# Stick-breaking attention layer: the first projections in rounds of 256 tokens, and q of the first half before k and v of the second

## The chip, the cores and the metric

The kernel runs on one core of a Trainium2 chip. The metric is the device time of one execution in microseconds. Before the change it is 693.96 us, the median of three runs (693.77 to 694.22).

## What is computed

One layer of a trunk with 1024 tokens and width 1024, all in float32:

```python
h = x * rsqrt(mean(x * x, -1) + eps) * norm_g
q, k, v, gate = split(h @ w_in, 4)              # 16 heads of 64
z = q @ k.T / 8
log_beta = log_sigmoid(z)
log_1m = where(key < query, log_beta - z, 0)
after = reverse exclusive cumsum of log_1m over keys
a = where(key < query, exp(log_beta + after), 0)
o = (a @ v) * silu(gate)
x = x + o @ w_out
out = x * rsqrt(mean(x * x, -1) + eps) * final_g
```

## The kernel before

The 16 heads are taken as 8 pairs. The engines run programs of their own, joined by semaphores; in each program a pair is 16 slots, and in the slots of one pair k, v, q and the gate of the next pair are projected in between. TensorE (PE) multiplies in a rounded float32 format; to keep precision each operand is split into a high and a low half, and a product is three matmuls (high by high, high by low, low by high).

Before the slots lies a prologue. It makes hT, the scaled and transposed input, of the eight x blocks of 128 tokens, and projects k, v and q of the first pair, 512 tokens ("a half") at a time.

- **Loads.** SP loads the odd x blocks and the w pieces (L374 to L382, two pieces of 4 x 128 rows for each of k, v, q), ACT the even x blocks (L672). Raw w always lies in w_raw, which has room for two pieces, so that a piece waits for the split of the one two before it (L361).
- **Scaling.** ACT squares blocks 0, 2, 4, 6, 7 (L684) and DVE 1, 3, 5 (L886), each with a sum along the row. A root is taken for blocks 0 to 3 and one for 4 to 7: ACT's square root (L676) and six small DVE instructions (rsqrt, L866). Blocks 3, 6 and 7 are scaled on ACT (L703), the others on DVE (L892).
- **hT.** PE transposes four blocks at a time, 128 columns each, into one of four PSUM banks (transpose_x, L511: 16 units, 8 of each half). ACT writes the high half with the gain (hi_x, L691), DVE the low half (lo_x, L897). A bank is free for unit n when unit n-4's low half is done.
- **Weights.** DVE casts the high half of each piece (next_w, L905), POOL subtracts it from the raw one for the low half (lo_w, L1109).
- **Projections.** In the order of PROLOGUE (L145): k, v of half 0, k, v of half 1, q of both. Each is 8 blocks of 3 matmuls of 512 columns (project, L494), in turns in proj_ps and o_ps. Units 4 to 7 are transposed between the blocks of the first, 8 to 15 between those of the second. ACT copies each result to stage (to_stage, L727), in program order with all its other work; projection h waits until result h-2 is there (L531). DVE splits k and q out of stage (heads_hi, heads_lo, L932, L942), and PE transposes v from there (transpose_v, L502), behind the third and the fifth projection.
- **PE's warm-up.** WARM_UP transposes of the identity (L524) run behind ACT's first square, ahead of the x transposes.
- **Slot 0** (L611): its own part of a projection first, then the scores (L578), which wait for all of q and k and for the copy of k with its heads swapped (swap_k, L366).

The planner at the top (plan, L38) and the order of slots are not touched.

## Time and profile before

| what | us |
|---|---|
| median of 3 runs | 693.96 (693.77 to 694.22) |
| the profiled execution, its own time | 693.87 |
| its span, first to last instruction | 692.1 |
| PE, DVE, ACT, POOL busy | 670.1, 480.0, 426.2, 280.2 |
| mean granted TensorE clock | 0.997 |

The profile is one execution. Times in its rows count from the start of the span. PE is a matmul, PEld its weight load; matmuls are pipelined, so that a row's duration is longer than its share of a stream. An idle time in brackets stands before the instruction, with what ended it.

### The profile page before, as it was taken

How to read it: one execution, taken by the hardware profiler on the slowest of the kernel's cores; microseconds unless marked ns; L12 is line 12 of the kernel's file. 1: busy time of each engine (PE TensorE's matmuls, PEld its weight loads, DVE VectorE, ACT ScalarE, POOL GpSimd, SP SyncE). 2: the span in 40 equal slices, each digit the busy share in tenths (PEclk: the TensorE clock that was granted, in tenths of full speed). 3: DMA queues.
4: the chain of work that ended last, by engine and by line, in shares of the span. 5: the costliest groups of instructions: out<-in, count | busy, mean ns of one | idle time of the engine just before them, and what ended most of it. 6: DMA issues, size and time to landing. Idle time of an engine off the chain costs nothing.

```text
span 692.1 us, 10879 instructions
## 1 busy us (share of the span) xinstructions
PE 670.1 (97%) x3426; PEld 563.5 (81%) x3426; DVE 480.0 (69%) x637; ACT 426.2 (62%) x795; POOL 280.2 (40%) x225
## 2 busy tenths in 40 slices
PE   5999999999999999999999999999999999999995
PEld 5787888888888888888888888888888777887784
DVE  5835666786778667766776677777776799644765
ACT  5614667676767676766676667666767685532432
POOL 2122435454454445544545363626353643324200
PEclk9999999999999999999999999999999999999998
DMA  7131311141115100420042014111421179222432
GB/s 289 46 90 48 92 31 31 55 129 33 31 30 139 46 19 30 121 76 15 30 122 63 28 32 121 61 31 30 121 62 30 61 239 320 96 92 65 162 124 91
DMA packets 28123, 57.65 MB, mean 83 GB/s; under 512 B 3376, under 2 KB 3376, under 8 KB 28080
## 3 DMA queue, kind: packets, MB, share of 16 engines
q1 hardware_dynamic: 25312, 51.13, 24.3%
q10 hardware_dynamic: 2736, 6.03, 2.3%
q8 instruction: 16, 0.26, 0.2%
q14 instruction: 27, 0.22, 0.1%
q0 software_dynamic: 32, 0.00, 0.0%
HBM read 37.23 MB, written 11.53 MB: 70 GB/s over the span
## 4 chain that ended last, share of the span: by engine, by line
PE 89%; DVE 6%; ACT 1%; issue 1%; DMA 1%; POOL 0%; POOLq 0%; ACTq 0%; DVEq 0%
PE proj_ps L497 46%; PE o_ps L643 10%; PE z_ps L592 9%; PE t_ps L655 9%; PE z_ps L572 6%; PE proj_ps L572 4%; PE o_ps L497 2%; DVE rest L1035 2%; PE t_ps L506 1%; PE z_ps L525 1%; DVE hT L901 1%; DMA a_group<-x 1%; DVE gate L1017 1%; PE z_ps L517 1%; DVE arena L981 1%
## 5 line engine op out<-in xcount | busy, mean ns | idle before, releaser
L497 PE MATMUL proj_ps<-hT,w_split 128*128 128x512 f32 x1464 | 359.9, 394 | 2.1 <-DVE hT L901 1.4
L497 PEld LDWEIGHTS proj_ps<-hT,w_split 128*128 128x128 f32 x1464 | 269.9, 188 | 57.6 <-DVE hT L901 2.3
L1136 POOL TENSOR_TENSOR a_group<-a_group,rest 128x128 f32<-128x128 f32 (+7 forms) x128 | 158.0, 1234 | 302.1 <-DVE rest L1035 302.1
L1035 DVE TENSOR_TENSOR_SCAN rest<-rest,restart 128x128 f32<-128x128 f32 (+7 forms) x128 | 204.4, 1597 | 16.4 <-ACT rest L820 16.0
L805 ACT ACTIVATE aT<-t_ps 128x512 fp32r<-128x512 f32 (+2 forms) x160 | 80.0, 531 | 62.8 <-PE t_ps L655 61.4
L1001 DVE TENSOR_TENSOR aT<-t_ps,aT 128x512 fp32r<-128x512 f32 (+2 forms) x160 | 93.0, 606 | 36.9 <-ACT aT L805 35.4
L1112 POOL TENSOR_TENSOR w_split<-w_raw,w_split 128x512 fp32r<-128x512 f32 x64 | 91.6, 1432 | 37.9 <-DVE w_split L863 37.9
L592 PE MATMUL z_ps<-arena 128*128 128x512 f32 (+2 forms) x384 | 96.4, 366 | 0.3 <-DVE arena L950 0.3
L950 DVE TENSOR_TENSOR arena<-stage,arena 64x512 fp32r<-64x512 f32 x64 | 43.9, 686 | 67.9 <-ACT arena L750 67.3
L820 ACT ACTIVATE rest<-z_ps 128x128 f32<-128x128 f32 (+7 forms) x128 | 83.8, 655 | 9.6 <-PE z_ps L592 9.3
L643 PE MATMUL o_ps<-aT,arena 128*128 128x512 f32 (+2 forms) x320 | 82.6, 364 | 2.8 <-DVE aT L1001 2.8
L822 ACT ACTIVATE a_group<-z_ps 128x128 f32<-128x128 f32 (+7 forms) x128 | 84.3, 659 | 0.0
L655 PE MATMUL t_ps<-ident,a_group 128*128 128x128 f32 x576 | 83.7, 272 | 0.5 <-POOL a_group L1136 0.5
L655 PEld LDWEIGHTS t_ps<-ident,a_group 128*128 128x128 f32 x576 | 69.2, 141 | 8.8 <-issue 0.9
L730 ACT ACTIVATE stage<-proj_ps 128x512 f32<-128x512 f32 x61 | 36.5, 599 | 61.0 <-PE proj_ps L497 61.0
L643 PEld LDWEIGHTS o_ps<-aT,arena 128*128 128x128 f32 x320 | 59.7, 188 | 17.5 <-DVE aT L1001 4.8
L592 PEld LDWEIGHTS z_ps<-arena 128*128 128x128 f32 x384 | 59.6, 190 | 5.2 <-DVE arena L950 0.8
L572 PE MATMUL z_ps<-arena,hT 128*128 128x512 f32 x246 | 58.4, 392 | 0.9 <-DVE a_group L1081 0.6
L797 ACT ACTIVATE oT<-o_ps 64x512 f32<-64x512 f32 x32 | 19.0, 593 | 59.5 <-PE o_ps L643 59.5
L572 PEld LDWEIGHTS z_ps<-arena,hT 128*128 128x128 f32 x246 | 45.5, 188 | 11.0 <-POOL arena L314 1.9
L991 DVE TENSOR_TENSOR oT<-o_ps,oT 64x512 f32<-64x512 f32 x32 | 22.0, 688 | 25.2 <-ACT oT L797 24.9
L757 ACT ACTIVATE w_split<-w_raw 128x512 fp32r<-128x512 f32 x56 | 35.9, 641 | 0.5
(89 smaller groups left out, 458.1 us busy)
## 6 DMA issues: line engine op xcount, KB each, us to landing
w_raw<-w_in SPq DMA_DIRECT2D x64, 256.0 KB, 2.6
arena<-arena SPq DMA_DIRECT2D x32, 256.0 KB, 4.3
wo_raw<-w_out SPq DMA_DIRECT2D x16, 256.0 KB, 3.9
o_hi_scratch<-o_split SPq DMA_DIRECT2D x14, 256.0 KB, 2.1
o_lo_scratch<-o_split SPq DMA_DIRECT2D x14, 256.0 KB, 2.4
hT<-o_hi_scratch SPq DMA_DIRECT2D x14, 256.0 KB, 5.8
hT<-o_lo_scratch SPq DMA_DIRECT2D x14, 256.0 KB, 6.5
a_group<-x SPq DMA_DIRECT2D x13, 256.0 KB, 3.3
```

Source lines behind the costliest of these rows:

```text
L497: mm = nc.tensor.matmul(bank[:, :], w_split[:, ring, wl, b, :], hT[:, hl, b, half * HALF:(half + 1) * HALF], start=(b == 0 and n == 0), st ...
L572: mm = nc.tensor.matmul(bank[:, :], hT[:, ol, b, tokens], w_out_of(nh, wl)[:, b, :], start=(b == first and m == 0), stop=(b == last and m ...
L592: mm = nc.tensor.matmul(z[:, c0:c1], q, k_of(par, hh, swapped)[:, c0 - first:c1 - first], start=not swapped, stop=swapped)
L643: mm = nc.tensor.matmul(o_ps[:, c:HALF], v_of(apar)[:, j, 2 * ahh:2 * ahh + 2, :] .rearrange("p x d -> p (x d)"), moving, start=(j == 0 an ...
L655: last = nc.tensor.transpose(t_ps[t % 2][:, i2 * P:(i2 + 1) * P], a_g[grp][:, i2, j * P:(j + 1) * P], ident[:, :])
L805: nc.scalar.activation(to, t_ps[t % 2][:, rel * P:HALF], ACT.Copy).then_inc(t_hi, 1)
L820: nc.scalar.activation(rest[:, s % 2, S - width:S], z_ps[s % 2][:, first:first + width], ACT.Sigmoid, scale=-SCALE).then_inc(rest_ready, 1)
L822: nc.scalar.activation(a_g[grp][:, i % GQ, 0:width], z_ps[s % 2][:, first:first + width], ACT.Sigmoid, scale=SCALE).then_inc(beta_ready, 1)
L1001: nc.vector.tensor_tensor(lo, t_ps[t % 2][:, rel * P:HALF], hi.bitcast(F32), ALU.subtract).then_inc(t_lo, 1)
L1035: nc.vector.tensor_tensor_scan(span, span, restart[:, S - 1:(S - 1 - width if width < S else None):-1], 0.0, ALU.mult, ALU.max).then_inc(s ...
L1112: nc.gpsimd.tensor_tensor(to[:, 1], w_raw[:, part, :].rearrange("p (b n) -> p b n", b=4), to[:, 0].bitcast(F32), ALU.subtract).then_inc(w_ ...
L1136: nc.gpsimd.tensor_tensor(a, a, rest[:, s % 2, S + 1 - width:S + 1], ALU.mult).then_inc(a_ready, 1)
```

## The change

- **Two rounds of 256 tokens.** The first half's units are now 16, of two blocks and 256 columns each (X_UNITS); the second half's stay 8 of four blocks. PE projects k, then v of tokens 0 to 255, then k, then v of tokens 256 to 511, with 256-wide matmuls, then q of half 0, and after that k, v, q of half 1. Units 4 to 15 stand between the blocks of the rounds, units 16 to 23 between those of q.
- **Three roots.** Blocks 0 and 1, 2 and 3, 4 to 7 have a root each. Block 1 is squared on DVE and scaled on ACT, block 2 squared and scaled on DVE, block 3 squared and scaled on ACT. The small instructions of the second root stand one by one between low halves of units 4 to 7.
- **Weights.** v's raw pieces are loaded into stage, q's are split into a quarter of the arena that is free until then. ACT casts k's first piece; SP and ACT load w pieces between the x blocks.
- **PE.** The warm-up has 54 transposes and doesn't wait for a square; 4 more (STILL_WARM) follow the first four units. The transpose of v's second half moves behind slot 0's own projection.
- **k swap.** It waits for three splits instead of two, since q's now stands between those of k.
- **Memory.** The buffer rest is allocated behind ident; what lay between shifts by its size.

The diff, cut to its core (a "..." is left-out lines):

```diff
-PROLOGUE = (("k", 0), ("v", 0), ("k", 1), ("v", 1), ("q", 0), ("q", 1))
-
-X_ACT, X_DVE = (3, 6, 7), (0, 1, 2, 4, 5)
+PROLOGUE = (("k", 0), ("v", 0), ("q", 0), ("k", 1), ("v", 1), ("q", 1))
+ROOTS = 3
+
+X_ACT, X_DVE = (1, 3, 6, 7), (0, 2, 4, 5)
 X_SCALED = [(1, X_ACT.index(b) + 1) if b in X_ACT else (0, X_DVE.index(b) + 1) for b in range(KB)]
-WARM_UP = 34
+WARM_UP = 54
+STILL_WARM = 4
+
+
+X_UNITS = [(b, 0, 2) for b in range(KB)] + [(b, 2, 2) for b in range(KB)] + [(b, GQ, GQ) for b in range(KB)]
+UNITS_X = len(X_UNITS)
...
-        rest = sb("rest", [P, 2, S + 1])
...
         ident = sb("ident", [P, P])
+        rest = sb("rest", [P, 2, S + 1])
...
+        wq_split = arena[:, 1, 3, :].rearrange("p (l b n) -> p l b n", l=2, b=KB)
+
+        def first_raw(n):
+
+            home = stage[:, n % 2, :] if n in (2, 3) else w_raw[:, n % 2, :]
+            return home.rearrange("p (b n) -> p b n", b=4)
+
+        def first_w(n):
+
+            unit, part = n // 2, n % 2
+            to = wq_split if unit == 2 else w_split[:, unit % 2]
+            return to[:, 0, 4 * part:4 * part + 4, :], to[:, 1, 4 * part:4 * part + 4, :]
+
+        def x_unit(u):
+
+            b, first, count = X_UNITS[u]
+            return b, slice(first * P, (first + count) * P), z_banks[u % 4][:, 0:count * P]
...
+        def load_first_w(eng, n):
+
+            eng.dma_start(first_raw(n).rearrange("p b n -> p (b n)"), w_in[(KB, 2 * KB, 0)[n // 2], n % 2, :, :]
+                          ).then_inc((wv_loaded if n in (2, 3) else w_loaded)[n % 2], 16)
+
+        def wait_first_w(eng, n):
+
+            if n in (2, 3):
+                eng.wait_ge(wv_loaded[n % 2], 16)
+            else:
+                eng.wait_ge(w_loaded[n % 2], 16 * max(n // 2, 1))
...
-                sp.wait_ge(qk_split, 4 * p + 2)
+                sp.wait_ge(qk_split, 4 * p + (3 if is_first(p) else 2))
...
-            for b in (1, 3):
+            load_x_block(sp, 1)
+            load_first_w(sp, 0)
+            load_x_block(sp, 3)
+            for n in (2, 3):
+                load_first_w(sp, n)
+            for b in (5, 7):
                 load_x_block(sp, b)
-
-            kinds = (1, 2, 0)
-            for n in range(2 * UNITS0):
-                load_w(n, n % 2, n % 2, kinds[n // 2] * KB)
-                if n == 1:
-                    for b in (5, 7):
-                        load_x_block(sp, b)
+            for n in (4, 5):
+                sp.wait_ge(w_ready, n - 3)
+                load_first_w(sp, n)
...
+            def transpose_x(u):
+                b, first, count = X_UNITS[u]
+                wait(pe, xt_lo, u - 3)
+                for i in range(count):
+                    scaled, done = X_SCALED[first + i]
+                    pe.wait_ge((x_scaled, x_scaled_act)[scaled], done)
+                    last = nc.tensor.transpose(z_banks[u % 4][:, i * P:(i + 1) * P],
+                                               x_blocks[first + i][:, b * P:(b + 1) * P], ident[:, :])
...
+            def project_first(unit, bank, cols, b):
+
+                weights = wq_split if unit == 2 else w_split[:, unit]
+                for n, (wl, hl) in enumerate(((0, 0), (0, 1), (1, 0))):
+                    mm = nc.tensor.matmul(bank, weights[:, wl, b, :], hT[:, hl, b, cols],
+                                          start=(b == 0 and n == 0), stop=(b == KB - 1 and n == 2))
+                return mm
...
-            pe.wait_ge(x_squared, 1)
             for n in range(WARM_UP):
                 nc.tensor.transpose(z_banks[0][:, 0:P], ident[:, :], ident[:, :])
-            for n in range(4):
-                transpose_x(n)
+            for u in range(4):
+                transpose_x(u)
+            for n in range(STILL_WARM):
+                nc.tensor.transpose(t_ps[0][:, 0:P], ident[:, :], ident[:, :])
+
+            for quarter in range(2):
+                for unit, bank in enumerate((proj_ps, o_ps)):
+                    cols = slice(quarter * 2 * P, (quarter + 1) * 2 * P)
+                    for b in range(KB):
+                        pe.wait_ge(xt_lo, KB * quarter + b + 1)
+                        pe.wait_ge(w_ready, 2 * unit + b // 4 + 1)
+                        mm = project_first(unit, bank[:, cols], cols, b)
+                        if quarter == 0 and b // 4 == unit:
+                            transpose_x((4, 8)[unit] + b % 4)
+                        if quarter == 1 and unit == 0 and b < 4:
+                            transpose_x(12 + b)
+                    if quarter == 1:
+                        mm.then_inc(proj_done, 1)
...
+                if h < 2:
+                    continue
                 wait(pe, stage_ready, h - 1)
                 for b in range(KB):
-                    pe.wait_ge(xt_lo, KB * half + b + 1)
-                    pe.wait_ge(w_ready, 2 * unit + b // 4 + 1)
-                    mm = project(unit % 2, (proj_ps, o_ps)[h % 2], half, b)
-                    if h == 0 and b < 4:
-                        transpose_x(b + 4)
-                    if h == 1:
-                        transpose_x(KB + b)
+                    pe.wait_ge(xt_lo, 2 * KB + (b + 1 if half else 0))
+                    pe.wait_ge(w_ready, 2 * "kvq".index(kind) + b // 4 + 1)
+                    mm = project_first("kvq".index(kind), (proj_ps, o_ps)[h % 2][:, :],
+                                       slice(half * HALF, (half + 1) * HALF), b)
+                    if h == 2:
+                        transpose_x(2 * KB + b)
                 mm.then_inc(proj_done, 1)
-                if h in (2, 4):
-                    transpose_v(h // 2 - 1, h // 2 - 1, h - 1, 1)
+                if h == 2:
+                    transpose_v(0, 0, 1, 1)
...
+                        pe.wait_ge(xt_lo, UNITS_X)
...
                     project_part(p, s)
+                    transpose_v(1, 1, 4, 0)
...
-            for b in range(0, KB, 2):
+            for b in (0, 2):
+                load_x_block(act, b)
+            load_first_w(act, 1)
+            for b in (4, 6):
                 load_x_block(act, b)
...
+            def hi_x(u):
+                b, cols, bank = x_unit(u)
+                act.wait_ge(xt_done, u + 1)
+                nc.scalar.activation(hT[:, 0, b, cols], bank, ACT.Copy, scale=g_col[:, b:b + 1]).then_inc(xt_hi, 1)
+
+            def scale_x(b, number):
+
+                act.wait_ge(rstd_ready, 5 * number)
+                nc.scalar.activation(x_blocks[b], x_blocks[b], ACT.Copy, scale=rstd[:, b:b + 1]
+                                     ).then_inc(x_scaled_act, 1)
+
+            def hi_first_w(n):
+
+                wait_first_w(act, n)
+                nc.scalar.activation(first_w(n)[0], first_raw(n), ACT.Copy).then_inc(w_hi, 1)
...
             square_x(0, 0)
-            square_x(1, 2)
+            act.wait_ge(x_squared_dve, 1)
+            root(slice(0, 2), x_squared, 1)
+            hi_first_w(0)
+            scale_x(1, 1)
+            act.wait_ge(g_loaded, 16)
+            for u in range(4):
+                hi_x(u)
+            square_x(1, 3)
+            hi_x(4)
             act.wait_ge(x_squared_dve, 2)
-            root(slice(0, 4), x_squared, 2)
+            root(slice(2, 4), x_squared, 2)
+            for u in range(5, KB):
+                hi_x(u)
             square_x(2, 4)
-
-            def scale_x(blocks):
-                for b in blocks:
-                    nc.scalar.activation(x_blocks[b], x_blocks[b], ACT.Copy, scale=rstd[:, b:b + 1]
-                                         ).then_inc(x_scaled_act, 1)
-
-            act.wait_ge(rstd_ready, 5)
-            scale_x(X_ACT[:1])
-            act.wait_ge(g_loaded, 16)
-            for n in range(KB):
-                hi_x(n)
-                if n in (3, 4):
-                    square_x(n, n + 3)
-                if n == 5:
-                    act.wait_ge(x_squared_dve, 3)
-                    root(slice(4, 8), x_squared, 5)
-            act.wait_ge(rstd_ready, 10)
-            scale_x(X_ACT[1:])
+            scale_x(3, 2)
+            for u in range(KB, 2 * KB):
+                hi_x(u)
+                if u == KB + 3:
+                    square_x(3, 6)
+            act.wait_ge(x_squared_dve, 4)
+            root(slice(4, 8), x_squared, 4)
+            scale_x(6, 3)
+            scale_x(7, 3)
...
+                if h in (2, 4, 5):
+                    act.wait_ge(qk_split, {2: 1, 4: 2, 5: 3}[h])
+                if h < 2:
+                    act.wait_ge(w_ready, 3 + h)
+                if h == 3:
+                    act.wait_ge(t_done, 1)
                 to_stage((proj_ps, o_ps)[h % 2], h, h % 2)
-                if h == 0:
-                    for n in range(KB, 2 * KB):
-                        hi_x(n)
-                if h in (3, 5):
-                    v_hi(0, h // 2 - 1, h // 2 - 1, h // 2 - 1)
+                if h == 1:
+                    for u in range(2 * KB, UNITS_X):
+                        hi_x(u)
+                    v_hi(0, 0, 0, 0)
...
+            v_hi(0, 1, 1, 1)
...
-                        act.wait_ge(qk_split, 3 + half)
+                        act.wait_ge(qk_split, 4)
+                        act.wait_ge(t_done, 2)
...
+            def next_w(n):
+                wait_first_w(dve, n)
+                nc.vector.tensor_copy(first_w(n)[0], first_raw(n)).then_inc(w_hi, 1)
...
             square_x(0, 1)
-            square_x(1, 3)
             dve.wait_ge(table_loaded, 1)
+            dve.wait_ge(x_squared_dve, 1)
+            dve.wait_ge(x_squared, 1)
+            rsqrt(slice(0, 2), 0)
+            scale_x(X_DVE[:1])
+            square_x(1, 2)
+            dve.wait_ge(g_loaded, 16)
+            for u in range(4):
+                lo_x(u)
+                if u in (1, 3):
+                    next_w((u + 1) // 2)
+            dve.wait_ge(x_squared, 2)
             dve.wait_ge(x_squared_dve, 2)
-            dve.wait_ge(x_squared, 2)
-            rsqrt(slice(0, 4), 0)
-            scale_x(X_DVE[:3])
-            next_w(0)
-            next_w(1)
-            dve.wait_ge(g_loaded, 16)
-            for n in range(KB):
-                lo_x(n)
-                if n == 2:
-                    square_x(2, 5)
-                    next_w(2)
-                if n == 3:
+            root_of_second = rsqrt_steps(slice(2, 4), 1)
+            for u in range(4, KB):
+                next(root_of_second)
+                lo_x(u)
+                if u == KB - 3:
                     next_w(3)
-                if n == 6:
-                    dve.wait_ge(x_squared, 5)
-                    dve.wait_ge(x_squared_dve, 3)
-                    rsqrt(slice(4, 8), 1)
-            scale_x(X_DVE[3:])
+            for _ in root_of_second:
+                pass
+            scale_x(X_DVE[1:2])
+            square_x(2, 5)
+            for u in range(KB, 2 * KB):
+                lo_x(u)
+                if u == KB + 3:
+                    square_x(3, 7)
+                if u in (KB + 5, KB + 6):
+                    next_w(u - KB - 1)
+            dve.wait_ge(x_squared, 4)
+            dve.wait_ge(x_squared_dve, 4)
+            rsqrt(slice(4, 8), 2)
+            scale_x(X_DVE[2:])
...
             for h, (kind, half) in enumerate(PROLOGUE):
-                if h in (2, 4, 5):
+                if h == 1:
+                    for u in range(2 * KB, UNITS_X):
+                        lo_x(u)
+                        if u == 2 * KB + 2:
+                            heads_hi("k", 0, 0, 0, 0)
+                            heads_lo("k", 0, 0, 0, 1)
+                    v_lo(0, 0, 0, 0)
+                if h in (2, 3, 5):
                     heads_hi(kind, 0, half, h, h % 2)
-                    heads_lo(kind, 0, half, h % 2, {2: 2, 4: 3, 5: 4}[h])
-                if h in (3, 5):
-                    v_lo(0, h // 2 - 1, h // 2 - 1, h // 2 - 1)
-                if h in (2, 3):
-
+                    heads_lo(kind, 0, half, h % 2, {2: 2, 3: 3, 5: 4}[h])
+                if h == 4:
                     dve.wait_ge(proj_done, h + 1)
-                    next_w(2 * h)
-                    next_w(2 * h + 1)
+                    next_w(2 * UNITS0)
+                    next_w(2 * UNITS0 + 1)
+            v_lo(0, 1, 1, 1)
...
             def wo_hi_part(n):
                 wait_wo(dve, n)
@@ -1088,7 +1184,7 @@
                 nc.vector.tensor_tensor(ssq[:, b:b + 1], ssq[:, b:b + 1], ssq[:, n:n + 1], ALU.add
                                         ).then_inc(ssq_summed, 1)
                 dve.wait_ge(ssq_summed, b + 1)
-                rsqrt(slice(b, b + 1), 2 + b)
+                rsqrt(slice(b, b + 1), ROOTS + b)
                 dve.wait_ge(y_weighted, 2 * b + 2)
                 nc.vector.tensor_scalar(out_of(b)[1], out_of(b)[1], rstd[:, b:b + 1], None,
                                         ALU.mult).then_inc(out_ready, 1)
@@ -1106,6 +1202,13 @@
             pool.wait_ge(consts_ready, 2)
```

## Rows read from the trace of the kernel before

**Rows 1.** Windows: us, length, busy PE PEld DVE ACT POOL, clock, DMA share, GB/s.

```profile
6.00:8.00 2.00, 0.99 (x5) 1.02 (x6) 0.77 (x2) 0.87 (x2) 0.00 (x0) 1.00 1.03 413
...
60.00:680.00 620.00, 614.78 (x3147) 517.50 (x3147) 440.65 (x551) 397.96 (x748) 267.39 (x208) 1.00 0.26 79
```

**Rows 2.** Windows of PE alone, otherwise as rows 1.

```profile
13.40:24.50 11.10, 9.66 (x58) 1.00 0.36 117
24.50:56.50 32.00, 32.00 (x162) 1.00 0.27 67
```

**Rows 3.** Timeline of PE: start, duration, instruction, idle before it.

```profile
7.01 6.55 PE L525 MATMUL z_ps<-ident 128*128 128x128 f32 x34 [7.01 <-ACT oT L688]
13.40 1.91 PE L517 MATMUL z_ps<-ident,a_group 128*128 128x128 f32 x16
...
56.51 2.88 PE L497 MATMUL proj_ps<-hT,w_split 128*128 128x512 f32 x12
59.74 0.50 PE L592 MATMUL z_ps<-arena 128*128 128x256 f32 x2 [0.34 <-DVE arena L950]
```

**Rows 4.** The chain that ended last: start, us, what (the DVE stretch from 14.90 ends in the first).

```profile
23.13 0.76 DVE hT L901
...
24.90 0.69 PE o_ps L497 x3
25.59 0.44 PE z_ps L517 x4
...
39.84 5.47 PE o_ps L497 x24
```

**Rows 5.** Timeline of DVE and POOL in the first 24 us.

```profile
16.89 1.22 DVE L889 CUSTOM_DVE_ANT_0 gate<-a_group 128x1024 f32<-128x1024 f32 x1
18.03 0.42 DVE L863 CAST w_split<-w_raw 128x512 fp32r<-128x512 f32 x1
18.36 0.74 DVE L901 SCALAR_TENSOR_TENSOR hT<-z_ps,g_col,hT 128x512 fp32r<-128x512 f32 x1
18.53 1.29 POOL L1112 TENSOR_TENSOR w_split<-w_raw,w_split 128x512 fp32r<-128x512 f32 x1 [2.24 <-DVE w_split L863]
19.02 1.07 DVE L863 CAST w_split<-w_raw 128x512 fp32r<-128x512 f32 x1
20.02 2.05 DVE L901 SCALAR_TENSOR_TENSOR hT<-z_ps,g_col,hT 128x512 fp32r<-128x512 f32 x3
22.00 0.15 DVE L869 TENSOR_SCALAR mean_sq<-ssq 128x4 f32<-128x4 f32 x1
```

**Rows 6.** Timeline, 74 to 92 us: widths of 512 and 256.

```profile
75.10 0.69 DVE L1001 TENSOR_TENSOR aT<-t_ps,aT 128x512 fp32r<-128x512 f32 x1
83.72 0.43 DVE L1001 TENSOR_TENSOR aT<-t_ps,aT 128x256 fp32r<-128x256 f32 x1
...
90.91 0.40 PE L643 MATMUL o_ps<-aT_pad,arena 128*128 128x256 f32 x2
```

**Rows 7.** Timeline of ACT in the first 26 us.

```profile
14.10 2.42 ACT L694 ACTIVATE hT<-z_ps,g_col 128x512 fp32r<-128x512 f32 x4 [1.45 <-PE z_ps L517]
16.39 1.08 ACT L688 ACTIVATE oT<-rest 128x1024 f32<-128x1024 f32 x1
23.12 2.19 ACT L705 ACTIVATE rest<-rest,rstd 128x1024 f32<-128x1024 f32 x2 [1.85 <-DVE rstd L880]
```

**Rows 8.** The identity on POOL; warm-up by source, two windows (ns min/median/max, first and last start).

```profile
2.41 0.29 POOL L1103 TENSOR_SCALAR_AFFINE_SELECT ident<-ident 128x128 f32<-128x128 f32 x1 [0.24 <-POOL ident L1101]
...
L525 PE MATMUL z_ps<-ident x3: 317/421/421, 11.9 to 12.4; 128*128 128x128 f32 x3
L525 PE MATMUL z_ps<-ident x4: 272/272/273, 13.0 to 13.3; 128*128 128x128 f32 x4
```

**Rows 9.** Timeline of POOL and DVE near 123 us.

```profile
123.02 2.01 POOL L1136 TENSOR_TENSOR a_group<-a_group,rest 128x1024 f32<-128x1024 f32 x1 [2.30 <-DVE rest L1035]
123.65 1.93 DVE L1017 TENSOR_TENSOR gate<-stage,gate 128x512 f32<-128x512 f32 x1 [0.77 <-ACT gate L787]
```

63 lines of the change are left out of this document (24 added, 39 removed).

## Prediction

> **What bounds the kernel now.** I read the stretches first. From 60 to 680 us TensorE (PE) is busy for 614.78 of 620 us, DVE, the next, for 440.65 [rows 1]. In front of that PE is busy from 24.5 to 56.5 us 32.00 of 32.00, but from 13.4 to 24.5 us only 9.66 of 11.10 [rows 2]. The slots behind 59.74 us are not touched by the change, and a PE that is never idle there can neither catch up nor hide anything. So the time is decided by one number: when PE starts the first score matmul of slot 0, now at 59.74 us [rows 3].
>
> Ahead of it PE idles until 7.01 us, runs 34 warm-up transposes and starts the x transposes at 13.40; from the first v matmuls, in the chain at 24.90 us [rows 4], nothing holds it until slot 0, whose third-quarter projection starts at 56.51 and whose scores wait 0.34 us for the last q split [rows 3]. The chain of waits says why the first part is slow: between 14.90 and 23.93 us it runs through DVE alone (low halves of h, a square, casts of w, six small root instructions, the last low half at 23.13) [rows 4, 5].
>
> **Unit prices.** On PE three 512-wide matmuls take 0.69 and four transposes 0.44 us (1.13 us for a block with both), 24 matmuls 5.47 [rows 4]. Two 256-wide matmuls are 0.24 apart from what follows (90.91 to 91.15), so three of them cost 0.35 and two transposes 0.22 us [rows 6]. On DVE a 512-wide low half advances the queue by 0.66 us (three from 20.02 to 22.00), a square by 1.14 (16.89 to 18.03), a cast by 0.33 (18.03 to 18.36), the six small root instructions by 1.13 (22.00 to 23.13) [rows 5]. Half as wide, an evacuation costs 0.26 us less on DVE (0.69 against 0.43) [rows 6]: so 0.40 for a low half; for ACT I take 0.2 less: from four high halves in 2.42 us (0.6 each, some 0.7 until one is done) it is 0.4 of queue and 0.5 until done. ACT: square 1.08, two scalings 2.19 [rows 7]; an evacuation to stage counts as a 512-wide high half without its gain, 0.6. POOL's low half of w: 1.29 [rows 5].
>
> **What the change adds, removes and moves.**
> 1. Warm-up: 54 transposes instead of 34, no longer behind the first square but behind the identity, which POOL finishes at 2.70 us [rows 8]. Now 24 of them run at the lower level (421 ns each, some 0.22 apart), and at 12.3 us, 5.3 us after the start, they turn to 272 ns and 0.11 apart [rows 8]; the profile's granted clock reads 1.00 all along, so it is these durations that tell 1.2 from 2.4 GHz. I take the same 5.3 us: 24 slow (5.3) and 30 fast (3.3) from 2.75 give a first x transpose T0 at 11.3, against 13.40: 2.1 us earlier. Blocks 0 and 1 are no bound: squares end at 6.9 as now, the small chain takes 1.4 with the wait for ACT's root (estimate: the 1.13 and one ACT instruction of the same size), ACT's scaling 1.1: 9.5 us. When the clock turns is the loosest term: T0 comes 0.9 us earlier or 0.8 later if the turn comes a third sooner or later than 5.3 us (3.5: 16 slow and 38 fast; 7.0: 32 and 22). That third is a choice of mine, since the rows hold a single turn.
> 2. Extra PE work: 4 more transposes (0.44) and 192 matmuls of 256 for 96 of 512, 32 x 0.35 - 16 x 0.69 = 0.2 us. The 4 lie in the wait for the first low half, the rest in waits for DVE, below.
> 3. The first 512 tokens now pass in two rounds of 256. DVE, which is the chain now, still has the same sum but pays fixed parts twice: 16 halves at 0.40 for 8 at 0.66 is 6.4 for 5.3 us, and there are three root chains for two. And all of x blocks 4 to 7 is scaled behind the last low half of round two.
> 4. Transposing v's second half moves from between v and q (0.44 on PE) behind the projection of slot 0, where 0.34 of it falls into the old wait. The score start is then 12 x 0.228 + 0.44 = 3.2 us behind the end of q, as now (59.74 - 56.51).
> 5. Weights: k as before; v's raw rows in stage, q's split in a free quarter of the arena. Only q's load waits for w's first splits. ACT takes over one cast (0.7 as a high half) and one scaling (1.1) before 9.5 us, under the warm-up. The order of loads: SP issues x1, w0, x3, v0, v1, x5, x7, ACT x0, x2, w1, x4, x6. At 413 GB/s for both queues [rows 1] a 512 KB block takes 2.5 us of a queue and a 256 KB piece 1.3; the first blocks are there some 1.3 us, a square with its sum, ahead of PE's release at 7.01 [rows 3, 7]: 5.7. So w0 lands near 7.0, x3 at 9.5, v0 at 10.8, v1 at 12.0, x5 at 14.6, x7 at 17; they are wanted at 7.1, 13.1, 14.2, 16.2, 19.5 and 23.7. Cost 0; w0 may come 1.8 us late, which the warm-up covers. The k swap starts behind the third split instead of the second and needs its 3 to 5 us before slot 0: it has over 6.
> 6. Behind the first scores ACT has v's high half (0.6) in front of the sigmoid table load; about half of it is new delay, and the first slots' ACT work has little slack: 0 to 0.3, left in the range.
> 7. Moved rest buffer: every buffer between its places shifts, none changes size. No row shows a cost: 0, bound plus or minus 0.5 us.
>
> **The sum, along the new chain.** From T0: two transposes (0.4), hi (0.48): first low half at 12.25. Two of them and the cast of w1 end at 13.4; POOL takes w1's low half from 13.5 to 14.8. A DVE cast that meets it is held: now the one at 19.02 took 1.07 for 0.42 us and ended 0.27 behind POOL [rows 5]. So the cast of v0 (due at 14.2) starts at 14.65. Low halves 4 to 7, v1's cast and the root chain of blocks 2 and 3 give 3.1 us: 18.1. Here two small two-input instructions meet POOL's v1 part (16.6 to 17.9). A two-input DVE instruction is held as well: 1.93 us for gate's product while POOL ran from 123.02 to 125.03 [rows 9]; no row shows a small one beside POOL. Bounds: 0 and 0.7; I take 0.7, since both kinds that are seen are held: 18.8. Scale x3 on ACT, 19.95; but PE, with k's last block at 18.5 and five v blocks (0.35 each), puts the first transpose of round two at 20.65. Its low half starts at 21.6; four are paced by PE at 0.57 (0.35 + 0.22): 23.7. Square of x7: 24.85. Two low halves, q0's cast, one low half: 26.4. q1's cast is held by POOL's q0 part (26.1 to 27.4): 27.6. Last low half 28.0. The root chain of blocks 4 to 7 meets POOL's q1 part (27.7 to 29.0): bounds 0 and 0.85, taken 0.85: 28.85 + 1.13 = 30.0. ACT scales x6 and x7 (2.2), and only then moves k's first half to stage (0.6), which frees the bank q needs: **q starts at 32.8**.
>
> From there PE is the bound as today: 8 x 1.13 + 0.44 + 3 x 5.47 = 25.9 us. Counted back from 56.51, today's order equals a q start at 30.6. So 32.8 - 30.6 = 2.2, less 0.05 from item 4: **+2.1 us**. The profiled execution took 693.87 us (span 692.1), 0.09 below the median of 693.96; 693.87 + 2.1 gives 696.0 for either, to the rounding. A difference of 0.2%, 1.4 us, is about what a measurement of this kernel can tell from none.
>
> The Trainium skill, SBUF — State Buffer, section "Who interferes with whom", says that a DVE instruction with two SBUF inputs, or in a two-port mode, and a GpSimd one that reads SBUF exclude each other for the whole of the first. The two held rows agree; by that rule the small chains are held (+2.1), by what rows show of small instructions alone they need not be (+0.6).
>
> **Rivals.**
> - *Small chains not held.* 1.55 us less: q at 31.2, +0.6, 694.5; with T0 from 10.4 to 12.1, 693.6 to 695.4. For it: these instructions last 0.16 us. Against: both held kinds. 0.28.
> - *PE alone sets the rounds: faster.* If DVE and ACT keep pace with 256-wide pieces, PE needs from T0 only 16 x 0.22 + 4 x 0.11 + 32 x 0.35 = 15.2: q at 26.5, 4.1 us before the neutral 30.6, 689.8. It turns faster by over 0.2% once q starts before 29.2, that is if over 3.6 of my 6.3 us of waits vanish. For it: 2.1 us at the start are sure. Against: DVE alone is the chain in half this work today [rows 4]. 0.12, with its partial forms.
> - *The clock falls.* In rounds one and two PE has 15.2 us of work in 21.5 us, and around 14 to 19 us under half. If it drops to 1.2 GHz for v's first quarter, its 8 x 0.35 + 4 x 0.22 = 3.7 us of work double, most of it on the chain: about +3 more, 699. Against: 9.66 of 11.10 us kept full rate. 0.06.
> - *Nothing:* waits and head start cancel by other sums, 694.0. 0.04.
>
> **Numbers.** Forecast (small chains held) 0.50: T0 alone spreads it over 695.1 to 696.8. The range 693.3 to 697.3 takes in the first rival and the address term, and leaves out the faster rival and the falling clock. Slower: nine tenths of the forecast, the clock, a little of the first rival: 0.52. Faster 0.12. Same 0.36.
>
> **What would show it.** First x transpose at 10.4 to 12.1 us; casts of v0 and q1 near 1 us long; a DVE root instruction longer than 0.4 us beside POOL; last root chain ending near 30, ACT stage right behind two scalings, first 512-wide q matmul at 32.8, first score at 61.9; PE busy without a gap between. I am wrong if q starts before 30.6, if PE transposes there last 421 ns, or if the slots from 62 us on take another time than now.

## The result, and the profile after

The changed kernel takes 698.83 us (median of 4 runs, 698.29 to 702.84) against 693.87 for the kernel before (median of 4, 693.59 to 694.22): ratio 1.0083 [1.0055, 1.0111], slower. The forecast was 696.0, with a range up to 697.3. The profiled execution of the changed kernel took 698.29 us, with a span of 696.5 (692.1 before), so 4.4 us are to be found in it. (The median lies 0.5 us above this execution, in the kernel before 0.0; the medians are 4.96 us apart.)

First the stretches that answer to [rows 1, 2]: us, length, busy time of PE, PEld, DVE, ACT and POOL, granted clock, DMA share, GB/s.

```profile
6.00:8.00 2.00, 2.00 (x12) 2.00 (x11) 1.48 (x7) 1.77 (x4) 0.00 (x0) 1.00 1.02 414
13.40:24.50 11.10, 9.56 (x78) 8.88 (x75) 9.73 (x23) 7.64 (x17) 3.85 (x3) 1.00 0.32 119
24.50:56.50 32.00, 30.56 (x165) 26.12 (x164) 20.39 (x39) 12.56 (x21) 4.82 (x4) 0.95 0.19 49
60.00:680.00 620.00, 610.54 (x3135) 514.61 (x3134) 436.69 (x544) 396.61 (x744) 266.46 (x208) 1.00 0.26 78
```

In the last of them TensorE is busy 4.24 us less than before (610.54 for 614.78), although the change has nothing there. The timeline of PE shows both places, the new prologue and the slots:

```profile
2.76 8.58 PE L570 MATMUL z_ps<-ident 128*128 128x128 f32 x54 [2.76 <-POOL ident L1199]
11.18 1.04 PE L555 MATMUL z_ps<-ident,a_group 128*128 128x128 f32 x8
...
28.31 1.01 PE L563 MATMUL proj_ps<-hT,w_split 128*128 128x256 f32 x3 [1.02 <-DVE hT L989]
29.11 4.20 PE L563 MATMUL o_ps<-hT,w_split 128*128 128x256 f32 x24
33.15 0.86 PE L563 MATMUL proj_ps<-hT,arena 128*128 128x512 f32 x3
...
61.70 0.60 PE L544 MATMUL t_ps<-ident,stage 128*128 128x128 f32 x4
62.19 0.74 PE L653 MATMUL z_ps<-arena 128*128 128x256 f32 x4
...
268.62 3.03 PE L535 MATMUL proj_ps<-hT,w_split 128*128 128x512 f32 x12 [2.08 <-ACT stage L806]
...
411.72 2.56 PE L535 MATMUL proj_ps<-hT,w_split 128*128 128x512 f32 x10 [2.06 <-ACT stage L806]
```

The first x transpose is at 11.18, q starts at 33.15, and the first score at 62.19 instead of 59.74 [rows 3]: +2.45 us, close to the forecast. But in the slots TensorE now waits twice, 2.08 and 2.06 us, for an evacuation by ScalarE. That evacuation in the timeline of ACT:

```profile
263.96 1.02 ACT L901 ACTIVATE a_group<-z_ps 128x1024 f32<-128x1024 f32 x1
267.97 0.60 ACT L806 ACTIVATE stage<-proj_ps 128x512 f32<-128x512 f32 x1 [2.98 <-issue]
...
411.07 0.60 ACT L806 ACTIVATE stage<-proj_ps 128x512 f32<-128x512 f32 x1 [2.97 <-issue]
...
580.00 0.60 ACT L806 ACTIVATE stage<-proj_ps 128x512 f32<-128x512 f32 x1
```

and in that of the kernel before:

```profile
261.83 1.02 ACT L822 ACTIVATE a_group<-z_ps 128x1024 f32<-128x1024 f32 x1
263.65 0.60 ACT L730 ACTIVATE stage<-proj_ps 128x512 f32<-128x512 f32 x1 [0.80 <-PE proj_ps L497]
...
574.26 0.60 ACT L730 ACTIVATE stage<-proj_ps 128x512 f32<-128x512 f32 x1
```

ScalarE idles for 3 us, and the profile puts that down to issue: nothing that it shows was waited for. Both evacuations are the first work of a turn of the loop over pairs (two pairs a turn, 143 us), the second and the third turn.

The whole account, from the same evacuation in both kernels and from the ends: first score +2.45; the two waits +4.14; between them everything gets a little shorter, since the last evacuation is +5.74 (580.00 for 574.26) where 2.45 + 4.14 = 6.59 stand, so -0.85; -0.09 up to the issue of the last store by SyncE (693.30 for 687.65, +5.65); and behind that issue 3.2 us for 4.45, -1.25. The sum is 4.4. Only the first of the terms is the prologue's timing; the experiments below show what the others come from.

### The profile page after: what moved, and what is told of

Its sections match the earlier page's. It is cut to its first block, busy times and chain, and to the rows that moved or that the text cites. A ratio compares the mean times of both kernels' runs of the same rounds, so it can differ in the third digit from the quotient of the medians.

```text
span 696.5 us, 11073 instructions
## 1 busy us (share of the span) xinstructions
PE 674.4 (97%) x3498; PEld 570.5 (82%) x3498; DVE 481.6 (69%) x651; ACT 428.7 (62%) x804; POOL 280.1 (40%) x225
## 4 chain that ended last, share of the span: by engine, by line
PE 88%; DVE 6%; issue 2%; ACT 2%; POOL 1%; POOLq 0%; ACTq 0%; DVEq 0%
PE proj_ps L535 43%; PE o_ps L705 10%; PE z_ps L653 9%; PE t_ps L717 8%; PE z_ps L633 6%; PE proj_ps L633 3%; PE o_ps L563 3%; PE proj_ps L563 2%; DVE rest L1131 2%; PE z_ps L570 1%; PE t_ps L544 1%; DVE hT L989 1%; PE z_ps L555 1%; DVE gate L1113 1%; ACT stage L806 1%
## 5 line engine op out<-in xcount | busy, mean ns | idle before, releaser
L535 PE MATMUL proj_ps<-hT,w_split 128*128 128x512 f32 x1392 | 341.7, 394 | 4.9 <-ACT stage L806 4.8
L535 PEld LDWEIGHTS proj_ps<-hT,w_split 128*128 128x128 f32 x1392 | 257.1, 188 | 57.2 <-ACT stage L806 5.3
L705 PE MATMUL o_ps<-aT,arena 128*128 128x512 f32 (+2 forms) x320 | 81.1, 359 | 2.8 <-DVE aT L1097 2.8
L1215 POOL TENSOR_TENSOR w_split<-w_raw,w_split 128x512 fp32r<-128x512 f32 x56 | 80.3, 1434 | 0.0
```

Of the source, the lines that this page charges most:

```text
L535: mm = nc.tensor.matmul(bank[:, :], w_split[:, ring, wl, b, :], hT[:, hl, b, half * HALF:(half + 1) * HALF], start=(b == 0 and n == 0), st ...
L705: mm = nc.tensor.matmul(o_ps[:, c:HALF], v_of(apar)[:, j, 2 * ahh:2 * ahh + 2, :] .rearrange("p x d -> p (x d)"), moving, start=(j == 0 an ...
L1215: nc.gpsimd.tensor_tensor(to[:, 1], w_raw[:, part, :].rearrange("p (b n) -> p b n", b=4), to[:, 0].bitcast(F32), ALU.subtract).then_inc(w_ ...
```

## The experiments

### Where ScalarE's loop lies

The four kernels of this group add only waits on a semaphore that has long been reached, in idle time of ScalarE. Two such waits make one instruction. The edit of the first, in ScalarE's loop over PROLOGUE, ahead of the fourth stage ("..." is left-out lines):

```
+            def idle_act(n):
+                for _ in range(n):
+                    act.wait_ge(consts_ready, 2)
...
+                if h == 3:
+                    idle_act(32)
```

The expectations count where ScalarE's loop begins in its program: at instruction 187 in before, 199 in the changed kernel. The trace holds some ten instructions fewer ahead of the loop, and the same differences: 12 more in the changed kernel than in before, and 16, 160, 12 and 4 more by the added waits.

**Before, 16 instructions more (32 waits).**

> The kernel before, with 32 waits on a semaphore that is long reached put into ScalarE's program in the prologue, ahead of the fourth stage (two waits make one instruction, so 16 instructions; they stand in an idle wait of ScalarE of 4 to 5 us). No work is added and no other engine's program changes. In before the loop over pairs begins at ScalarE's instruction 187, in the changed kernel at 199, here at 203. Theory F (the two new stalls of 2.1 us at the back edge of ScalarE's loop come from where its loop lies in its instruction stream): two stalls of about 2.1 us at ScalarE's first evacuation of the loop's second and third turn, near 263 and 405 us, with an idle time of ScalarE of about 3 us put down to issue; the span grows by 4.1 us, 698.0 against 693.9 (ratio 1.006). Rival D (the stalls come from the changed data flow or timing: q late, v's transpose late, weight loads): no stall, 693.9 (ratio 1.000).

693.45 us, ratio 0.9997 [0.9988, 1.0006], no wait. As stated, theory F fell: a stream that is merely longer, or a loop merely behind some threshold, doesn't stall.

**Changed, 160 instructions more (320 waits over three stages).**

> The changed kernel, with 320 waits on a semaphore that is long reached (160 instructions) in ScalarE's prologue, spread over its idle waits ahead of the last three stages, so that its loop begins at instruction 359 instead of 199. Theory F, with pages of 256 instructions of which two are at hand: the loop's 409 instructions lie in two pages again, both stalls of 2.1 us are gone, 694.7 against 698.8 for the changed kernel (ratio to before 1.0015); if the 160 waits take longer than ScalarE's idle time there, up to 1 us is given back and it is 695.7. A theory in which what matters is only that ScalarE's stream became longer: both stalls stay or grow, 698.8 or more. Rival D: 698.8 (ratio 1.007).

693.93 us, ratio 1.0007 [0.9998, 1.0016]; both waits are gone, and with them 4.9 us, though nothing else was altered. So the place does matter: the data flow is the same, and the stalls are gone. (Of the 4.9 us some 0.85 may be the prologue's own scatter: its first score was that much sooner in the profiled execution, where the 54 warm-up transposes ended at 10.4 instead of 11.2, and the clock stayed at 1.00 in v's quarter.) What would join both results is a window of places. The profile of the kernel before lists two queues of instruction packets. The second, q14, moved 27 packets with 0.22 MB, some 8 KB each, and it is its packets that come at other times when ScalarE's or VectorE's program is longer:

```profile
q8 instruction: 16, 0.26, 0.2%
q14 instruction: 27, 0.22, 0.1%
```

So ScalarE's program is taken to arrive in blocks of 8 KB. With the loop's start at 187 (before) and 203 harmless and at 199 harmful, the guess was that at 199 the end of such a block lies between the loop's start and its first evacuation, a few instructions on. Two kernels test it from both sides.

**Before, 12 instructions more (24 waits).**

> The kernel before with 24 waits on a semaphore long reached (12 instructions) in ScalarE's prologue, so that its loop over pairs begins at exactly the instruction number of the changed kernel's. At shift 16 nothing happened. Theory F2 (the loop's first instructions lie across the end of a block of instructions that is fetched by itself, blocks of 8 KB by the instruction packets of the profile, so that the first evacuation of a turn waits for two fetches in a row instead of one; this holds for a few starting places in 128 only): both stalls of about 2 us appear at the first evacuation of the second and third turn, 697.6 against 693.5 (ratio 1.006). Rival D2 (it is the place together with something else in the changed kernel, its load on ScalarE's queue or its data flow): no stall, 693.5 (ratio 1.000).

698.75 us, ratio 1.0066 [1.005, 1.0081]: the kernel before, with twelve instructions that do nothing, is as slow as the changed one (three runs at 698.68 to 698.85, and one at 696.99 with a mean granted clock of 0.997 for their 0.995). The evacuation by source, what its engine idled for ahead of it (this kernel):

```profile
  PE proj_ps L497: 58.9, 56
  PE o_ps L497: 11.0, 2
  issue: 5.7, 2
```

Here 1.80 and 2.05 us of TensorE are the stalls (the timeline of PE):

```profile
265.95 4.61 PE L497 MATMUL proj_ps<-hT,w_split 128*128 128x512 f32 x12 [1.80 <-ACT stage L734]
...
410.92 1.43 PE L497 MATMUL proj_ps<-hT,w_split 128*128 128x512 f32 x5 [2.05 <-ACT stage L734]
```

Behind the first of them the granted clock fell (PE's windows: length, busy, count, clock, then the DMA share and GB/s):

```profile
264.00:266.00 2.00, 0.20 (x3) 1.00 0.02 4
266.00:268.00 2.00, 2.00 (x5) 0.54 0.00 0
268.00:270.00 2.00, 2.00 (x7) 0.61 0.51 131
```

TensorE had been busy for 0.20 of 2 us; the next twelve matmuls took 4.61 us, where 3.03 stand in the changed kernel at 268.62. The changed kernel's profiled execution kept 1.00 behind both of its stalls, with TensorE busy for 0.54 us from 266 to 268, so it has 4.1 us where this one has some 5.4 (1.80 + 2.05 + 1.58).

**Changed, 4 instructions more (8 waits).**

> The changed kernel with 8 waits on a semaphore long reached (4 instructions) in ScalarE's prologue. Theory F2: the end of the block lies ahead of the loop's first instruction, both stalls are gone, 694.5 against 698.8 (ratio to before 1.001). Rival (only a shift by most of a block, as the 160 of the run before, helps): both stalls stay, 698.6 (ratio 1.007).

693.61 us, ratio 1.0001 [0.9992, 1.001]: four instructions take 5.2 us off the changed kernel. Its timeline of ACT, to be set beside 263.96 and 267.97 above:

```profile
263.75 1.02 ACT L907 ACTIVATE a_group<-z_ps 128x1024 f32<-128x1024 f32 x1
265.65 0.60 ACT L810 ACTIVATE stage<-proj_ps 128x512 f32<-128x512 f32 x1 [0.89 <-PE proj_ps L535]
```

The evacuation is back to 1.9 us behind the last instruction of the turn, from 4.0. The instruction packets of q14 fit. Read in half microseconds around the first back edge (the jump from the end of a turn to the loop's start):

| kernel | packets from | evacuation at |
|---|---|---|
| before | 261.5, 264, 266 | 263.65 |
| before + 16 | 261.5, 263.5 | 263.37 |
| changed + 4 | 263.5, 266 | 265.65 |
| before + 12 | 261.5, 263.5, 265.5 | 265.30 |
| changed | 264, 266, 268.5 | 267.97 |

In the three kernels that don't stall the evacuation runs behind the first packet, in the two that do behind the second. Their number doesn't decide: before has three and no stall. The trace also holds the register instructions, which the views leave out, and they say it more sharply. The loop's body begins with two of them ahead of the evacuation. In the changed kernel they run at 265.56 and 267.88, at the second back edge at 408.85 and 410.98; in before + 12 at 263.15 and 265.21. In before they run at 263.43 and 263.54, and 0.11 us apart in the other kernels that don't stall. So the whole stall lies between the loop's first and second instruction. Each of the two runs some 1.5 us behind the start of a packet: 265.56 behind 264.03 and 267.88 behind 266.42 in the changed kernel, 265.21 behind 263.75 in before + 12. One fetch is thus nearly hidden, behind the running ACTIVATE and the wait for TensorE; the second, 2.1 to 2.4 us behind the first, isn't. That the place decides is shown by the runs; that it is the second fetch rests on these times, since the packets do not say whose they are.

The Trainium skill, Runtime: NRT & Kernel Launch, section "Instruction fetch mechanics", says that a taken branch to a target outside the two blocks at hand stalls until the block is fetched, and gives blocks of 16 KB and 256 instructions for all engines. The wait for a fetch behind the back edge is seen here. The size agrees for q8 (16 packets, 0.26 MB), which is taken to be TensorE's, and not for q14 (8 KB), where the measurement decides; by the page's 64 bytes an instruction (16 KB for 256) a packet of q14 would be 128 instructions, an estimate.

### How the chain of the prologue is held

**Changed, q1's cast later.**

```
-                if u in (KB + 5, KB + 6):
-                    next_w(u - KB - 1)
+                if u == KB + 5:
+                    next_w(4)
...
             scale_x(X_DVE[2:])
+            next_w(5)
```

> The changed kernel with VectorE's cast of q's second weight half moved from between the lo halves of rounds two to behind the last scale of x, so that GpSimd's 1.27 us subtraction of it doesn't meet the small instructions of the third root. Theory H (those small instructions are held by GpSimd's work, and the chain to the third round sets when q starts): the cast of 1.33 us leaves the chain and the mean is not held for 0.8 us; q starts 1.5 to 2.1 us earlier, at about 31.3 instead of 33.15, the first score at about 60.3 instead of 62.2; with both stalls of the loop left as they are, 696.9 against 698.8 (ratio to before 1.0045). Rival P (TensorE's own work, with v's second quarter at the lower clock, sets it): v's quarter ends at 33.0 with or without, q starts at 33.1, 698.6 (ratio 1.007).

697.39 us, ratio 1.0046 [1.0033, 1.006], 1.4 us off. The ten runs fall apart: four at 695.1 to 695.5, five at 697.4 to 698.1, one at 699.85; so the profiled execution (697.92) says more than the median. In it q starts at 31.45, the first score is at 60.58, 1.6 us sooner; both stalls of the loop are still there (1.88 and 1.90). Theory H holds. DVE in the changed kernel, with POOL beside it:

```profile
16.84 1.27 POOL L1210 TENSOR_TENSOR w_split<-stage,w_split 128x512 fp32r<-128x512 f32 x1 [0.36 <-DVE w_split L943]
17.14 0.98 DVE L958 TENSOR_TENSOR newton<-newton,mean_sq 128x2 f32<-128x2 f32 x1
...
26.53 1.33 DVE L943 CAST arena<-w_raw 128x512 fp32r<-128x512 f32 x1
27.94 1.28 POOL L1210 TENSOR_TENSOR arena<-w_raw,arena 128x512 fp32r<-128x512 f32 x1 [0.36 <-DVE arena L943]
28.17 1.07 DVE L948 TENSOR_SCALAR mean_sq<-ssq 128x4 f32<-128x4 f32 x1
```

and with the cast later:

```profile
27.05 0.69 DVE L948 TENSOR_SCALAR mean_sq<-ssq 128x4 f32<-128x4 f32 x1
```

A product of two columns takes 0.98 us, a one-input instruction on four columns 1.07, both until POOL is done. With the cast later the mean still takes 0.69 us, until POOL's first q part ends at 27.71: it is held for less, not free. Rival P fell too: TensorE had the time, it now waits 0.76 us for ScalarE's evacuation.

**That, the evacuation first, and the loop moved by 4.** The edit beside the two above, without the lines that take the first evacuation out of its old place:

```
             root(slice(4, 8), x_squared, 4)
...
+            act.wait_ge(w_ready, 3)
+            to_stage(proj_ps, 0, 0)
             scale_x(6, 3)
             scale_x(7, 3)
```

> The changed kernel with three edits: 4 instructions more on ScalarE (the loop's stalls go), VectorE's cast of q's second weight half behind the last scale of x, and ScalarE's first evacuation ahead of its scales of x6 and x7 instead of behind them. Theory H: q's start is set by VectorE's chain and by that evacuation; it starts when v's quarter is done and x7 is scaled enough for its transposes, at about 30.7 instead of 33.15 (31.45 with the cast alone), the first score at 59.9 against 62.2 and 59.7 in before; no stalls; with the short end and the moved buffer 691.7 (ratio to before 0.997). Rival P (TensorE's own work, 2 us more of it than in before, sets the first score once the chain is out of the way): q at 31.4, first score at 60.6, 692.5 (ratio 0.998). If the lower clock comes in v's quarter: 1 us more.

691.45 us, ratio 0.9966 [0.9953, 0.9978]: faster than both kernels. No stall, q at 29.51, first score at 58.55, 1.2 us ahead of before. The profiled execution is the fastest of the six, 0.9 us under their median. It beat the forecast of 59.9, and 0.9 to 1.0 us of that is the start: here the first low half of h starts at 11.36, in the changed kernel at 12.25 and in the one with the cast alone at 12.37. The 54 warm-up transposes end between 10.3 and 11.3 from execution to execution, while x1 is scaled at 9.6; what differs is when their spacing turns from 0.21 to 0.11 us, behind 15 of them here and behind 23 in the changed kernel.

**The same with 42 warm-up transposes.**

```
-WARM_UP = 54
+WARM_UP = 42
```

> The kernel of the three edits before, with 42 transposes of the identity ahead of TensorE's first x transpose instead of 54. x1 is scaled at 9.6 us, the 54 end at 10.3 to 11.3 from run to run. Theory W (the warm-up's own length holds the first x transpose, and VectorE's chain behind it carries this to the first score): at the 12 per us of the full clock it starts 1.0 us sooner, at 9.6 to 10.3, q and the first score 0.7 to 1.0 us sooner, 690.6 against 691.5 (ratio to before 0.9954). Rival C (the shorter warm-up leaves a stretch in which TensorE idles and the granted clock falls to 0.5 in the first or the second round): some 1 us lost there, 691.5 to 693. Rival N (the chain of VectorE waits for the weights or for x2 anyway): the first score is the same, 691.5 (ratio 0.9966).

689.88 us (5 runs, 689.78 to 690.17), ratio 0.9941 [0.9928, 0.9955], the fastest kernel of the study, 4.1 us under before. Its PE timeline:

```profile
2.76 6.64 PE L570 MATMUL z_ps<-ident 128*128 128x128 f32 x42 [2.76 <-POOL ident L1210]
9.23 1.24 PE L555 MATMUL z_ps<-ident,a_group 128*128 128x128 f32 x8
...
28.68 0.86 PE L563 MATMUL proj_ps<-hT,arena 128*128 128x512 f32 x3
...
57.73 0.74 PE L653 MATMUL z_ps<-arena 128*128 128x256 f32 x4
```

Theory W holds: the first x transpose is 1.1 us sooner than in the execution above (at 0.11 us apart 12 transposes are 1.3 us, not the 1.0 of the expectation), q another 0.8 us, and the clock did not fall.

### Where the buffers lie

**Before, rest buffer moved alone.**

```
-        rest = sb("rest", [P, 2, S + 1])
...
         ident = sb("ident", [P, P])
+        rest = sb("rest", [P, 2, S + 1])
```

> The kernel before with one line moved: the rest buffer is declared behind the identity, as in the change, so that aT, aT_pad, stage, gate, oT, o_split and ident lie 8,200 bytes lower. Theory L (the layout is what made the slots of the changed kernel a little shorter and its end shorter): the evacuations of proj_ps in the slots drift ahead of those of before by about 0.13 us per pair, 0.8 us by the last pair, and the stretch from the last store's issue to the end of the span is 3.2 us instead of 4.45; in all 691.9 us against 693.9 (ratio 0.997). If only the slots come from it: 693.1. Rival (the layout does nothing, the 0.8 and the 1.25 us come from the new prologue or from scatter): 693.9, ratio 1.000, and no drift.

692.74 us, ratio 0.9986 [0.9977, 0.9995]: 1.0 us faster. Against before, the evacuations drift from -0.27 us at 56 us to -1.18 at 573, the 0.9 us of the changed kernel. The stretch behind the last store is 4.4 us: that term has another cause. Matmuls of the slots by shape, 123 to 621 us (count, busy us, mean ns, idle before), in before

```profile
L497 PE MATMUL proj_ps<-hT,w_split 128*128 128x512 f32 x1200 | 294.5, 394 | 0.0
...
L643 PE MATMUL o_ps<-aT,arena 128*128 128x512 f32 x176 | 50.9, 398 | 1.3 <-DVE aT L1001 1.3
```

and with the buffer moved

```profile
L497 PE MATMUL proj_ps<-hT,w_split 128*128 128x512 f32 x1199 | 294.5, 394 | 0.0
...
L643 PE MATMUL o_ps<-aT,arena 128*128 128x512 f32 x176 | 49.9, 392 | 1.3 <-DVE aT L1001 1.3
```

The matmuls that read aT, which moved, are quicker: 6 ns each, 1.0 us in this window. No other row of the view moves by more than 0.3 us, but for one group whose count differs.

**Before, two gaps of 32 bytes.**

```
         rest = sb("rest", [P, 2, S + 1])
+        gap = [sb("gap0", [P, 8])]
...
         ident = sb("ident", [P, P])
+        gap.append(sb("gap1", [P, 8]))
```

> The kernel before with its order of buffers, and a gap of 32 bytes behind the rest buffer (which takes 8,224 bytes of each partition, 32 more than a multiple of 64) and one of 32 bytes behind the identity: aT, aT_pad, stage, gate, oT, o_split and the identity start at multiples of 64 bytes, as in the changed kernel, instead of 32 above one; no other buffer's residue changes, no instruction does. Theory A (what the moved buffer brings is the starting address, modulo 64, of the buffers that TensorE reads and the others that were behind it): the evacuations drift ahead by 0.13 us per pair as with the moved buffer, 692.8 (ratio to before 0.9986). Rival O (the place or order of the buffers, 8 KB up or down, brings it): no drift, 693.8 (ratio 1.000).

699.27 us, ratio 1.0079 [1.0065, 1.0093]: 5.5 us slower, which neither theory had, and my statement that no other residue changes was true for 64 only: w_split had gone 64 bytes further. The row names it:

```profile
L499 PE MATMUL proj_ps<-hT,w_split 128*128 128x512 f32 x1203 | 300.5, 397 | 0.0
```

**Before, w_split alone 64 or 32 bytes further** (a gap of 16 or 8 columns behind eps_col).

> The kernel before with a gap of 64 bytes ahead of w_split; no instruction and no other buffer moves. Theory M (the time of a matmul depends on the starting addresses of what it reads; the projections' weights 64 bytes further cost 4 ns each): mean of the projections' matmuls 398 ns instead of 394, some 1,500 of them, 698.9 against 693.8 (ratio 1.0075), the matmuls of o and z as in before. Rival G (the cost of the gaps came from aT, the stage or the small buffers): 394 ns, 693.8 (ratio 1.000).

> The same with a gap of 32 bytes. Theory M with a cost that grows by step: 396 ns, 696.3 (ratio 1.0037). Theory M with a cost that is had at 32 above a multiple of 64, or not: 394 ns and 693.8, or more than 398 ns and over 699. Rival G: 693.8.

698.63 us, ratio 1.0069 [1.0052, 1.0086], and 698.77, ratio 1.0074 [1.0057, 1.0091]; the row reads in the one and the other

```profile
L498 PE MATMUL proj_ps<-hT,w_split 128*128 128x512 f32 x1204 | 300.7, 398 | 0.0
```

```profile
L498 PE MATMUL proj_ps<-hT,w_split 128*128 128x512 f32 x1202 | 300.1, 398 | 0.0
```

### What is shorter at the end

**Changed + 4, one instruction more on SyncE.**

```
+            for _ in range(2):
+                sp.wait_ge(consts_ready, 2)
             swap_k(0, 0)
```

> The kernel with 4 more instructions on ScalarE, and one instruction more (two waits on a semaphore long reached) in SyncE's prologue, which brings SyncE's stream to before's 260 instructions (the change made it 259). Theory S (the 1.25 us shorter stretch behind the last store's issue comes from a fetch of a block of instructions that SyncE's closing part no longer needs): the stretch is 4.4 us again instead of 3.2, the span 1.2 us longer than without the extra instruction, 695.7 against 694.5. Rival T (the stretch comes from where the stores lie in their queues, or from another engine's stream): 3.2 us, 694.5.

694.13 us, ratio 1.0009 [0.9999, 1.0018]; span 692.5, last store issued at 689.27, so 3.2 us. Theory S fell.

**Before with the rest buffer moved, w1's load on ScalarE's queue.** The line that takes its place; SyncE's own load of that piece is gone:

```
+            act.dma_start(w_raw[:, 1, :], w_in[KB, 1, :, :]).then_inc(w_loaded[1], 16)
```

> The kernel before with the rest buffer behind the identity, and the load of k's second weight half moved from SyncE's to ScalarE's queue, behind x's blocks, so that SyncE's stream has 259 instructions. Theory S: the 1.0 us of the moved buffer, and the stretch behind the last store's issue at 3.2 us instead of 4.4: 691.5 (ratio 0.9968). Rival T: as with the moved buffer alone, 692.7 (ratio 0.9986). Either: the first score within 0.3 us of before's 59.74, unless k's second half comes too late for TensorE, which would add up to 1 us.

693.24 us, ratio 0.9994 [0.9985, 1.0003]; 4.4 us behind the last store: theory S fell a second time. The first score is at 60.09 instead of 59.47 with the buffer alone, so the later load costs 0.6.

**The same without that load, 15 instructions more on VectorE.**

```
+            for _ in range(30):
+                dve.wait_ge(consts_ready, 2)
             square_x(0, 1)
```

> The kernel before with the rest buffer behind the identity and 30 waits on a semaphore long reached (15 instructions) at the head of VectorE's program, where it is idle, so that VectorE's stream has the changed kernel's 609 instructions instead of 594. Theory V (the stretch behind the last store's issue is 1.25 us shorter in the changed kernel because the fetch of a block of VectorE's instructions, seen in the trace 1.8 us behind that issue, comes some instructions sooner): the stretch is 3.2 us instead of 4.4, the fetch is seen some 5 us ahead of the issue, and with the moved buffer's 1.0 us it is 691.5 (ratio to before 0.9968), faster than both kernels. Rival T (it is another engine's stream, TensorE's or GpSimd's, or the stores themselves): 4.4 us, 692.7 (ratio 0.9986).

691.86 us, ratio 0.9971 [0.996, 0.9982], also faster than both kernels. The last store is issued at 686.46, the span is 690.0: 3.5 us. The packet that stood 1.8 us behind that issue is now 5 us ahead of it, as expected. One more is left, at 690.3, some 0.3 us behind the last instruction of the span; before has it too. In the two kernels before whose ScalarE stream was 12 and 16 longer it is gone, VectorE's is left, and the stretch is 4.1 us. In the changed kernel both are ahead of the issue, and it is 3.2. So theory V holds for 0.9 of the 1.25 us, and the other 0.3 goes with the length of ScalarE's stream; how a packet that starts behind the last instruction could hold the end isn't shown.

## Why the prediction was wrong

Its time was 2.8 us short, although the term that it worked out was nearly right. Its direction came out right by luck: without the stalls of the loop, for which it had no term, the changed kernel is as fast as before (693.61 us, ratio 1.0001), since two gains, one that it put at nothing and one that it left out, cancel the loss in the prologue.

- **The step that failed** is the sentence on which the method stood: "The slots behind 59.74 us are not touched by the change". No instruction in them was, but the slots are a loop, and the number of instructions ahead of a loop is part of its timing. The change brought ScalarE's loop from instruction 187 to 199, and that costs 4.1 us (twelve idle instructions in before: +5.0 by the runs, with the fall of the clock; four in the changed kernel: -5.2). The prediction had no term for it; without it the time would lie inside the range. Its last line, on slots that "take another time than now", was the right alarm.
- **Item 7, the rest buffer:** 0 with a bound of 0.5 either way; it is -1.0 (before_rest). "No row shows a cost" was taken for no cost. The moved kernel's rows put it at the matmuls that read aT.
- **The end** had no term: -1.25. And the forecast was made for one execution 0.1 us from the median; in the changed kernel the profiled one lies 0.5 us below it.
- **Items 1 to 3, the chain:** item 2 counts twice the matmuls that there are (96 of 256 columns for 48 of 512), but its 0.2 us is reckoned from the right number. First x transpose 11.18 for 11.3; last root chain ends at 30.2 for 30.0; q at 33.15 for 32.8; ScalarE's evacuation right behind its two scalings, at 32.31. The small instructions were held, as the forecast took and the first rival denied: 0.98 and 1.07 us. The rule of the Trainium skill, SBUF — State Buffer, section "Who interferes with whom", covers the first; the second has one input of four columns and would be covered only in a two-port mode, which no row shows. That such small ones are held at all is what the rows add.
- **Items 4 to 6:** the first score is 3.2 us behind the start of slot 0's projection (62.19 for 58.97), as said; v's high half ahead of the table load shows no cost (the last evacuation ahead of the slots is +2.46, the first score +2.45).
- **The falling clock** came, but in v's second quarter, behind a wait of 1.02 us: granted 0.84, 0.50 (the 1.2 GHz level) and 0.81 in the stretches 27 to 29, 29 to 31 and 31 to 33 us, and 24 matmuls took 4.20 us, 3.03 where it held (the kernel with 160 instructions more). It cost some 0.2 us of the 2.45, since q had to wait until 32.9 for its bank anyway.
- **PE alone sets the rounds** was a real possibility, not reached by this order: with three small edits, q starts at 29.51, and at 28.68 with the shorter warm-up, against the neutral 30.6.

So the change alone, with its accident of places taken out, is worth nothing: 2.3 us lost in the prologue, 0.9 won by the buffer and 1.25 at the end (693.61). With the cast and the evacuation moved and the shorter warm-up it is worth 4.1 us, of which some 2 are the buffer and the end.

Open: how the spread of single runs (698.29 to 702.84 in the changed kernel, 695.11 to 699.85 with the cast later; 0.4 us in the fastest kernel) divides. Three things were seen to differ between executions: the length of the warm-up (1.0 us), the clock in v's quarter, and the clock behind a stall of the loop (1.6 us).

## What to carry to other kernels

A change in a prologue moves every loop behind it in its engine's stream, and a loop whose first instructions lie across the end of a fetched block costs 2 us at each jump back to its start: where a trace shows an engine idle for "issue" at the first instruction of a turn, shift the loop by a few idle instructions and measure before blaming the data flow. Try starts at multiples of 128 bytes for the buffers that matmuls read, and look at the mean time of each matmul shape when a buffer moves. Keep the small instructions of a chain out of the time of a GpSimd operation; one cast moved was worth 1.6 us.
